# Scores of three attention mixers: two low-factor passes stacked into one product over all 128 rows

## The reference

```python
def ab_mixer(x, w_in, w_out, sinks, t5_bias):          # layer 0
    qa, ka, va, qb, kb, vb = split(x @ w_in)
    ya = swa_sink_attention(qa, ka, va, sinks, t5_bias) # 8 heads, 2 kv heads, 128-key window
    yb = stick_breaking_attention(qb, kb, vb)           # 8 heads, all earlier keys
    return concatenate([ya, yb], axis=-1) @ w_out

def c_mixer(x, w_in, w_out, rel_table):                # layer 1
    q, k, v = split(x @ w_in, 3, axis=-1)
    return chunk_band_attention(q, k, v, rel_table) @ w_out  # 16 heads, own chunk + 8 chunks before
...
scores = einsum('...qd,...kd->...qk', q, k) * 64 ** -0.5     # in each of the three
```

## Time and profile before

| | us |
|---|---|
| median of three runs | 2420.47 (2416.39 to 2429.13) |
| the profiled execution | 2420.46 |
| its span | 2418.7 |
| PE busy in the span | 2313.3 |
| DVE busy | 1798.6 |
| ACT busy | 1370.5 |

### The profile page before, as it was taken

The page is one execution under the profiler, slowest core; times in us unless marked ns, Lnnn a source line. Parts: engine busy times, 40 slices in busy tenths (PEclk is TensorE's granted clock), DMA queues, the critical chain, the costliest instruction groups (busy, mean ns, idle before and its releaser), DMA issues. The chain is left out here.

```text
span 2418.7 us, 34192 instructions
## 1 busy us (share of the span) xinstructions
PE 2313.3 (96%) x12916; PEld 1887.0 (78%) x12916; DVE 1798.6 (74%) x2542; ACT 1370.5 (57%) x1686; POOL 273.9 (11%) x243
## 2 busy tenths in 40 slices
PE   8999998999999999998899999998989999999996
PEld 6777886887888888886677777776878888888883
DVE  4565556678999999997555455556689999999986
ACT  3454446126777777775344444444047777777763
POOL 0000000002212112111500000000011122111104
PEclk9999999999999999999999999999999999999998
DMA  4110003328999999999211111104159999999986
GB/s 127 28 32 27 27 10 85 145 105 350 389 387 376 386 386 383 389 387 338 93 47 43 41 38 38 38 36 168 44 200 406 397 398 398 387 380 378 373 332 244
DMA packets 156078, 534.40 MB, mean 221 GB/s; under 512 B 40160, under 2 KB 80120, under 8 KB 106760
## 3 DMA queue, kind: packets, MB, share of 16 engines
q1 hardware_dynamic: 136784, 498.46, 54.5%
q0 software_dynamic: 18496, 33.60, 3.7%
q10 hardware_dynamic: 632, 0.10, 0.0%
HBM read 515.23 MB, written 50.41 MB: 234 GB/s over the span
## 5 line engine op out<-in xcount | busy, mean ns | idle before, releaser
L367 DVE TENSOR_TENSOR arena<-arena,arena 128x2048 fp32r<-128x2048 f32 (+1 forms) x458 | 956.7, 2118 | 65.3 <-ACT arena L1991 50.3
L1991 ACT CAST arena<-arena 128x2048 fp32r<-128x2048 f32 x384 | 716.7, 1918 | 149.9 <-PE psum L1710 116.2
L1710 PE MATMUL psum<-arena,arena 128*128 128x512 f32 x3072 | 733.0, 394 | 0.0
L1710 PEld LDWEIGHTS psum<-arena,arena 128*128 128x128 f32 x3072 | 569.0, 189 | 114.3 <-issue 0.4
L664 PE MATMUL psum<-arena,arena 128*128 128x512 f32 x2016 | 506.1, 401 | 6.4 <-DVE arena L367 5.6
L664 PEld LDWEIGHTS psum<-arena,arena 128*128 128x128 f32 x2016 | 369.5, 189 | 100.5 <-issue 11.4
L1721 PE MATMUL psum<-arena,arena 128*128 128x512 f32 x1536 | 359.6, 390 | 2.8 <-DVE arena L367 2.8
L1721 PEld LDWEIGHTS psum<-arena,arena 128*128 128x128 f32 x1536 | 288.0, 188 | 64.0 <-DVE arena L367 4.1
L367 DVE TENSOR_TENSOR arena<-psum,arena 128x512 fp32r<-128x512 f32 (+1 forms) x186 | 160.5, 870 | 109.4 <-ACT arena L789 55.2
L806 ACT ACTIVATE arena<-arena,arena 128x640 f32<-128x640 f32 (+4 forms) x192 | 120.0, 626 | 203.5 <-DVE arena L904 152.8
L1207 PE MATMUL psum<-arena,arena 128*128 128x512 f32 x768 | 187.1, 399 | 9.3 <-ACT arena L363 6.9
(11 more groups left out here) (189 smaller groups left out, 1671.7 us busy)
## 6 DMA issues: line engine op xcount, KB each, us to landing
arena<-in_moe_w_gate SPq DMA_DIRECT2D x128, 1024.0 KB, 8.5
arena<-in_moe_w_up SPq DMA_DIRECT2D x128, 1024.0 KB, 7.6
arena<-in_moe_w_down SPq DMA_DIRECT2D x128, 1024.0 KB, 7.1
arena<-expert_rows SPq DMA_DIRECT2D x32, 512.0 KB, 11.2
x_rows<-arena SPq DMA_DIRECT2D x24, 512.0 KB, 2.6
arena<-in_c_w_in SPq DMA_DIRECT2D x24, 512.0 KB, 4.1
arena<-x_rows SPq DMA_DIRECT2D x24, 512.0 KB, 8.1
arena<-in_x SPq DMA_DIRECT2D x16, 512.0 KB, 7.0
```

Source lines behind the costliest of these rows:

```text
L367: return eng.tensor_tensor(tile, src, high.bitcast(F32), ALU.subtract)
L1710: mm = pe.matmul(bank(o), cs[:, c * P:(c + 1) * P], ws[:, c * FF:(c + 1) * FF], start=(k == 0 and c == 0), stop=(k == 2 and c == CH - 1))
L1991: act.copy(w_hi[w][:, cols], self.raw[w][:, cols]).then_inc(hi_ready[w], 1)
```

## The change

Each head gets tiles of all 128 partitions. `q_two[b][h]` holds, for head h, the low part of q on the head's own 64 partitions and the high part on the other 64; `k_two[kv][h]` holds the high part of k on the own and the low part on the other. One matmul over all 128 rows then makes low x high plus high x low for a head. The high x high pass stays a pair of half-row matmuls. For a piece: two half-row matmuls, then two full-row ones, in place of six half-row ones.

`q_hi` is now a tile for each pair, in the place where that pair's output will go later (with one exception per layer). ACT writes a Q half with three instructions and a K half with two, DVE writes each with two; the additional ones, and the K ones, cover 64 partitions each. For layer 0's last pair ACT first waits until all the weights are split. The third slot of the weights' high parts moves by 4 KB.

```diff
-            q_hi, q_lo = [pen(SEQ, F32R) for _ in range(2)], [pen(SEQ, F32R) for _ in range(2)]
-            k_hi, k_lo = [pen(SEQ, F32R) for _ in range(2)], [pen(SEQ, F32R) for _ in range(2)]
+            q_two, k_two = [[[pen(SEQ, F32R) for _ in range(2)] for _ in range(2)] for _ in range(2)]
...
+            q_homes = [place(AT_ROWS + 4 * n, SEQ, F32R) for n in range(8)]
+            if layer == 0:
+                q_homes[7] = place(WK, SEQ, F32R)
+            else:
+                q_homes[0] = place(WK + 8, SEQ, F32R)
...
+            def own(h):
+                return slice(DH * h, DH * (h + 1))
+
+            def other(h):
+                return own(1 - h)
+
+            def q_hi(n):
+
+                return q_homes[n]
...
                     for a, w in places[0][1]:
-                        for k, (qs, ks) in enumerate(((q_hi, k_hi), (q_lo, k_hi), (q_hi, k_lo))):
-                            for h in range(2):
-                                own = slice(DH * h, DH * (h + 1))
-                                at = places[h][0] + a
-                                done[h] = pe.matmul(psum[:, at:at + w], qs[b][own, t * P:(t + 1) * P],
-                                                    ks[kv][own, k0 + a:k0 + a + w], start=(k == 0), stop=(k == 2))
+                        keys = slice(k0 + a, k0 + a + w)
+                        into = [psum[:, places[h][0] + a:places[h][0] + a + w] for h in range(2)]
+                        qs = slice(t * P, (t + 1) * P)
+                        for h in range(2):
+                            pe.matmul(into[h], q_hi(pair.n)[own(h), qs], k_two[kv][h][own(h), keys],
+                                      start=True, stop=False)
+                        for h in range(2):
+                            done[h] = pe.matmul(into[h], q_two[b][h][:, qs], k_two[kv][h][:, keys],
+                                                start=False, stop=True)
...
                     if job.m == Q:
-                        act.mul(q_hi[b][:, cols], job_bank(i, g), DH ** -0.5).then_inc(hi_kept, 1)
+                        if layer == 0 and job.pair.n == len(plan.pairs) - 1:
+
+                            act.wait_ge(lo_ready, len(plan.jobs) - lead.early)
+                        act.mul(q_hi(job.pair.n)[:, cols], job_bank(i, g), DH ** -0.5)
+                        for h in range(2):
+                            ins = act.mul(q_two[b][h][other(h), cols], job_bank(i, g)[own(h), :], DH ** -0.5)
+                        ins.then_inc(hi_kept, 1)
                     elif job.m == K:
-                        act.copy(k_hi[kv][:, cols], job_bank(i, g)).then_inc(hi_kept, 1)
+                        for h in range(2):
+                            ins = act.copy(k_two[kv][h][own(h), cols], job_bank(i, g)[own(h), :])
+                        ins.then_inc(hi_kept, 1)
...
                     if job.m == Q:
-                        dve.scalar_tensor_tensor(out=q_lo[b][:, cols], in0=job_bank(i, g), scalar=DH ** -0.5,
-                                                 in1=q_hi[b][:, cols].bitcast(F32), op0=ALU.mult, op1=ALU.subtract
-                                                 ).then_inc(proj_kept, 1)
+                        for h in range(2):
+                            ins = dve.scalar_tensor_tensor(out=q_two[b][h][own(h), cols], in0=job_bank(i, g)[own(h), :],
+                                                           scalar=DH ** -0.5,
+                                                           in1=q_hi(job.pair.n)[own(h), cols].bitcast(F32),
+                                                           op0=ALU.mult, op1=ALU.subtract)
+                        ins.then_inc(proj_kept, 1)
                     elif job.m == K:
-                        split_lo(dve, k_lo[kv][:, cols], job_bank(i, g), k_hi[kv][:, cols]).then_inc(proj_kept, 1)
+                        for h in range(2):
+                            ins = split_lo(dve, k_two[kv][h][other(h), cols], job_bank(i, g)[own(h), :],
+                                           k_two[kv][h][own(h), cols])
+                        ins.then_inc(proj_kept, 1)
```

More of the change, by code:

```diff
@@ L526, in attention @@
             WK = AT_WORK
-            w_hi = first_w_hi + [place(WK + 32, CH * P, F32R)]
+            w_hi = first_w_hi + [place(WK + 36, CH * P, F32R)]
             w_lo = first_w_lo + [place(WK + 40, CH * P, F32R)]
```

## The result

The changed kernel takes 2495.5 us (median; 2487.5 to 2499.4), the kernel before 2421.8: ratio 1.0297, 95% interval 1.0278 to 1.0316. It is slower, as forecast, but by some 74 us where I said 49, and above the range that I gave (to 2487). The profiled execution's span grew from 2418.7 to 2491.8 us, by 73.1.

A forecast was written before the change was run, and what follows sets the result against it. PE, the tensor engine, was taken to bound nearly the whole kernel. 2420.5 us before, plus 19.2 for mode changes and 29.8 for waits on longer copy chains, gave 2469.5, taken as 2470 us; range 2448 to 2487 (8 in 10).

The forecast's parts named there:

- PE sets the time, a slot and a full-row product cost the same: Attention stages: PE bounds; two side-by-side half-row matmuls (a slot) cost 0.23 us, one full-row product 0.231, so no gain.
- Mode changes 19.2 us: Two-piece scores steps, stick-breaking pairs and layer 1: two more row-mode blocks, 0.4 us in each of 48 steps.
- The chain and its places: ACT and DVE copies before PE's next projection half: K 2.71, Q 3.20 us; waits in four stages sum to 29.8.
- the price of the copies: Each further 512-column copy in the chain adds 0.48 us on ACT and 0.60 on DVE, at full price despite 64 partitions.
- the upper bound: Copies without any overlap, 0.59 us on ACT and 0.69 on DVE: 12 us more over 40 halves, 42 in all.
- Two Vector instructions with no wait between them: Skill rule for DVE's new copies at partitions 0 and 64: second costs 0.69 us, not 0.60; sum grows 3.6 us.
- I charge them nothing: Work queued behind the copies (weight split, transposes' copies, exponentials, normalisation, bias step): 0 us, covered by a 3.0 us projection block.
- it spreads: Rival, chance 0.07: delayed exponentials reach the transposes, or the granted clock falls once or twice more; 71 us added, 2491.
- The late weights' DMA in layer 1's lead phase: Lead-phase copies were taken as hidden under projection blocks of 24 matmuls, 5.5 us, so nothing was charged there.
- The rest: All outside pairs 0 and 1, pairs 2 and 3, stick-breaking pairs and the layer 1 stretch: 1.6 us forecast growth.

The follow-up runs named there:

- B: The kernel before the change, with six half-row matmuls per piece of scores; median 2421.8 us.
- A: The changed kernel as described, with stacked tiles and no further edits, against the kernel before; median 2495.5 us, ratio 1.0297.

## Why the prediction was wrong

- *PE sets the time, a slot and a full-row product cost the same*: right. The form with grouped modes is B's time (ratio 1.0012).
- *Mode changes 19.2 us*: right. Put alone into B they add 19.6 us of span, 0.4 us in each step of two pieces. That taking them away from A gave 19 us back is no second proof: 11 us of that are theirs.
- *The chain and its places*: right as a mechanism. PE waits for L367 and L894 where I said, and with the bank freed early the waits after Q halves of layer 1 are gone.
- **The step that failed is the price of the copies.** The prediction put it: "two ACT casts of 512 columns back to back take 1.08 us, so a further one adds 0.48; two DVE subtractions from PSUM take 1.28, so a further one adds 0.60". The new copies start at partitions 0 and 64 in turn and add 0.60 and 0.70 (0.59 and 0.70 for K), the upper bound, which I had and did not take. By that Q's chain is 3.48 and K's 2.84 us. Over 28 Q and 12 K halves this is 28 x 0.28 + 12 x 0.13 = 9.4 us of the 24 missing, and in the stick-breaking pairs it is all that was missing (6 x 0.28 + 3 x 0.13 = 2.1). I had weighed the Trainium skill's "VectorE: DVE Perf Modes", section "Two Vector instructions with no wait between them", at 3.6 us and left it beside the sum. The traces agree with its rule for DVE (0.70 against 0.61). That ACT does the same stands on no row of before; the runs show it, and two of the Q chain's three held copies are ACT's.
- **The second step that failed** is "I charge them nothing", for what stands behind the copies, with the clock as it was. Even with the upper bound for the copies the sum is 2420.5 + 19.2 + 42 = 2482, 14 us short. I had this as the rival "it spreads" (2491), which takes that bound too, at 7%. With copies that overlap, A still stands at 2477, 7 us over my 2470. In pairs 0 and 1 the granted clock is 0.94, not 0.98, in pairs 2 and 3 0.91, not 0.95. As the lower level is half, 0.94 of 89.1 us is 10.7 us at it, against 3.0 before; 0.91 of 76.1 is 13.7 against 6.5. At half speed each such us costs up to 0.5: up to 3.8 and 3.6 us, of the 5.5 and 4.5 missing in these two stages. With the chains' 1.4 and 1.1 that comes to 5.2 and 4.7. The clock goes with the length of the chain, cut at the same projection matmuls: in pairs 0 and 1 it is 0.98 in the three kernels with B's copies and with the bank freed early, 0.96 with the copies over all 128 partitions, 0.94 to 0.96 in the five with A's copies in front of the bank. In pairs 2 and 3 it is less clear: 0.92 to 0.95, 0.95, 0.93, and 0.89 to 0.91. That is one profile each, and no run changes the clock alone. The late weights' DMA in layer 1's lead phase, which I passed over as hidden, can add up to 3.
- *The rest* (6.6 us outside the four stages, 1.6 forecast) is the second step of layer 1, 2.4 us longer up to the cut, and the end of the last pair and the expert stages, 6 us, less 1.1 us ahead of pair 0. The change doesn't touch the expert stages; with the modes grouped this end is 0.9 us longer than B's, with the bank freed early 8.4, so it varies from run to run. No run settles how much of it belongs to the change, and no single difference of a few us between two profiles is safe from it.

## What to carry to other kernels

Before stacking two half-row passes into one full-row product, look whether the halves already run side by side: here two 64-row matmuls on different rows start within 0.01 us of each other (1414.475 and 1414.479) and cost one slot, so stacking saves nothing. Count the changes of the array's row mode (0.2 us each) and keep one mode together over all pieces of a step. Price copies that stand in front of a single PSUM bank by their whole latency, without overlap where they start at other partitions than the one before, and let only those that must read the bank stand in the chain.

## What the runs showed of the hardware

- On ACT as on DVE, an instruction whose input or output starts at another partition than that of the one before (0 and 64 were tried) begins only when that one has ended: 512 columns then cost 0.60 us instead of 0.48 on ACT, and 0.70 instead of 0.61 on DVE. Either side alone does it.
- 64 partitions cost what 128 do: 0.59 and 0.60 us for 512 columns from PSUM on ACT, 0.69 and 0.69 on DVE.
- A change between half-row and full-row matmuls costs 0.2 us also inside one accumulation group in the same PSUM bank: two more changes made a step 0.4 us longer (form only, and modes grouped).
- What is taken out of PE's stream in front of a wait comes back as wait: the chain behind a Q half was 3.48 us with 0.41 us of idle time in front of PE's next half, and 3.47 us with 0.80.
